# Block 1's input projections reordered, the down projections' last weight piece taken late, and the last tiles finished from PSUM

## The reference

```python
h = rmsnorm(x, attn_norm[l])
c_q, c_kv, k_r, q_d, k_d, v_d = jnp.split(h @ w_in[l], split_at, axis=-1)
o_a = mla_mixer(c_q, c_kv, k_r, cos, sin, g_cq, g_ckv, w_uq, w_ukv, g_mla_q, g_mla_k)
q_d = rmsnorm(q_d.reshape(B, S, DIL_HEADS, DIL_HD), g_dil_q[l])
k_d = rmsnorm(k_d.reshape(B, S, DIL_HEADS, DIL_HD), g_dil_k[l])
o_b = dilated_attention(q_d, k_d, v_d, rel_bias)
x = x + jnp.concatenate([o_a, o_b], -1) @ w_out[l]
x = x + conv_ffn(rmsnorm(x, ffn_norm[l]), w_up[l], conv_w[l], conv_b[l], w_down[l])
```

```python
fx = rmsnorm_2(x, g_pre_ffn[i]) * (1.0 + sc2) + sh2
yx = conv_ffn_2(fx, w_up[i], w_ffn_conv[i], b_ffn_conv[i], w_down[i])
x = x + ga2 * rmsnorm_2(yx, g_post_ffn[i])
```

## Time and profile before

| | |
|---|---|
| three runs | 1769.87, 1771.72, 1773.66 us; median 1771.72 |
| profiled execution | 1769.04 us, of which the profile's span is 1767.3 us |
| granted TensorE clock, mean | 0.973 |
| busy share of the span | PE 93%, PEld 75%, DVE 64%, ACT 48%, POOL 15% |
| DMA | 258.32 MB, mean 146 GB/s |

### The profile page before, as it was taken

One profiled execution on the slowest core, in us unless ns is written; L12 is line 12 of the kernel. 1 busy time (PEld: TensorE's weight loads), 2 busy tenths in 40 slices (PEclk: granted clock), 3 DMA queues, 4 the chain that ended last, 5 costly groups with the idle time before them and its releaser, 6 DMA issues. The chain is left out here.

```text
span 1767.3 us, 22843 instructions
## 1 busy us (share of the span) xinstructions
PE 1639.4 (93%) x8628; PEld 1317.5 (75%) x8628; DVE 1124.4 (64%) x1875; ACT 848.6 (48%) x1518; POOL 262.0 (15%) x322
## 2 busy tenths in 40 slices
PE   7989999999999999899899899999999797989996
PEld 7667887886677887678467588888787595668875
DVE  5686898465868995553673744444333756579964
ACT  5554776355556664431353533333212534566742
POOL 2000113600021117000000001111630000001171
PEclk9999999999999999999999899999999799989998
DMA  7465765554578555523273533333222342246651
GB/s 261 151 209 172 202 189 180 193 167 166 198 225 246 145 170 169 161 78 96 94 237 111 155 96 96 96 96 96 96 95 96 102 138 66 72 124 187 184 185 48
DMA packets 266495, 258.32 MB, mean 146 GB/s; under 512 B 8821, under 2 KB 208729, under 8 KB 266130
## 3 DMA queue, kind: packets, MB, share of 16 engines
q1 hardware_dynamic: 262706, 245.36, 45.7%
q0 software_dynamic: 3536, 11.42, 1.8%
q10 hardware_dynamic: 144, 0.07, 0.0%
HBM read 255.72 MB, written 1.10 MB: 145 GB/s over the span
## 5 line engine op out<-in xcount | busy, mean ns | idle before, releaser
L556 PE MATMUL psv<-hHL,wH 128*128 128x512 f32 (+1 forms) x1952 | 644.2, 392 | 25.0 <-issue 21.1
L1186 DVE TENSOR_TENSOR wL<-ring,wH 128x1024 fp32r<-128x1024 f32 (+2 forms) x364 | 450.5, 1243 | 269.8 <-ACT wH L1761 266.7
L1761 ACT ACTIVATE wH<-ring 128x1024 fp32r<-128x1024 f32 (+2 forms) x364 | 376.1, 1040 | 302.1 <-PE psv L556 295.6
L556 PE MATMUL psv<-hHL,wL 128*128 128x256 f32 (+1 forms) x1504 | 468.5, 311 | 0.0
L556 PEld LDWEIGHTS psv<-hHL,wH 128*128 128x128 f32 x1952 | 368.2, 191 | 108.6 <-issue 23.3
L556 PE MATMUL psv<-wH,hHL 128*128 128x512 f32 (+2 forms) x936 | 319.2, 390 | 30.4 <-DVE wL L1186 17.6
L556 PEld LDWEIGHTS psv<-hHL,wL 128*128 128x128 f32 x1504 | 287.3, 191 | 15.9
L556 PE MATMUL pss<-wH,hHL 128*128 128x512 f32 (+3 forms) x808 | 274.4, 385 | 0.0
L556 PEld LDWEIGHTS psv<-wH,hHL 128*128 128x128 f32 x936 | 175.7, 189 | 74.4 <-DVE wL L1186 24.9
L556 PE MATMUL psv<-wL,hHL 128*128 128x512 f32 (+2 forms) x468 | 180.1, 385 | 0.0
L556 PEld LDWEIGHTS pss<-wH,hHL 128*128 128x128 f32 x808 | 152.5, 190 | 29.4
(11 more groups left out here) (239 smaller groups left out, 1702.3 us busy)
## 6 DMA issues: line engine op xcount, KB each, us to landing
ring<-in_w_up SPq DMA_DIRECT2D x176, 512.0 KB, 5.2
ring<-in_w_mod SPq DMA_DIRECT2D x96, 512.0 KB, 4.8
ring<-in_w_down SPq DMA_DIRECT2D x88, 512.0 KB, 4.3
ring<-in_w_in SPq DMA_DIRECT2D x52, 512.0 KB, 4.6
ring<-in_w_out SPq DMA_DIRECT2D x32, 512.0 KB, 4.7
ring<-in_w_in SPq DMA_DIRECT2D x8, 384.0 KB, 6.0
ring<-in_w_in SPq DMA_DIRECT2D x8, 288.0 KB, 6.9
ring<-in_w_ukv SPq DMA_DIRECT2D x4, 512.0 KB, 4.2
```

Source lines behind the costliest of these rows:

```text
L556: return pe.matmul(o, a, b, start=start, stop=stop, skip_group_check=True)
L1186: v.tensor_tensor(lo, raw, hi.bitcast(F32), ALU.subtract).then_inc(piece_split, told("piece_split", p))
L1761: return ac.activation(o, i, ACT.Copy)
```

## The change

Three things are rearranged; no arithmetic on weights or features is added or removed, apart from the last tiles.

*Input projections of block 1.* TensorE transposes the dilated heads before the bias bands and projection 4, not after them; the squares of the first 128 tokens' MLA heads get room in `W` of their own, so that ScalarE need not wait for the dilated heads. ScalarE splits the third piece of projection 2 ahead of the four latent squares, and does the roots for both tiles in one operation each. Both engines split the third piece of projection 4 earlier. ScalarE loads its Exp table before it empties projection 4. The first two pieces of the output projection are no longer split by VectorE before attention, but at steps p = 8 and 9 of it (`early`); ScalarE makes the first at p = 8 and the second behind its Sqrt table load, where it was. The modulation chunks for attention now come ahead of both `w_out` chunks in the load list.

*Down projections.* With `late`, the first two banks take pieces 19 and 20 before either takes piece 21.

*Last feed-forward.* For its two tiles the squares are summed and the gate is multiplied straight from PSUM, by halves, the updated rows come in halves (`finish`), and the output is stored by SP and ScalarE's queue instead of GpSimd's.

```diff
-        sqm = [w_at(14464, 16, MQK), view(scr, 0, 16, MQK)]
+        sqm = [w_at(10368, 16, MQK), view(scr, 0, 16, MQK)]
...
-            add_cols(A["w_out"][l], 0, 512, ph, "out", 0, between=lambda: add_mod(0, MOD1[l]["pairs"].values()))
+            add_mod(0, MOD1[l]["pairs"].values())
+            add_cols(A["w_out"][l], 0, 512, ph, "out", 0)
...
-            def piece_order(banks, n, tail):
+            def piece_order(banks, n, tail, late=False):
                 m = n - PIECES if tail else n
...
                         yield b, q, w
                     owed.append(piece_used)
                 ws = []
-                for i, b in enumerate(banks):
-                    for q in range(m, n):
-                        if len(ws) < n - m:
-                            ws.append(piece())
-                        yield b, q, ws[q - m]
-                        if i == len(banks) - 1:
-                            owed.append(piece_used)
+                turns = [(i, q) for i in range(len(banks)) for q in range(m, n)]
+                if late:
+                    turns = [(i, q) for i in (0, 1) for q in range(m, n - 1)] + [(0, n - 1), (1, n - 1)] + turns[2 * (n - m):]
+                for i, q in turns:
+                    if len(ws) <= q - m:
+                        ws.append(piece())
+                    yield banks[i], q, ws[q - m]
+                    if i == len(banks) - 1:
+                        owed.append(piece_used)
...
-                for (t, h, kind, b), j, w in piece_order(banks, NJ, True):
+                for (t, h, kind, b), j, w in piece_order(banks, NJ, True, True):
...
+                pe.wait_ge(dil_heads, at("dil_heads", ph))
+                for t in range(NT):
+                    for g in range(2):
+                        transposes("VS"[g], (ph, "dT", t, g),
+                                   [(dqk[:, t, 8 * g + 2 * k:8 * g + 2 * k + 2, :].rearrange("p a b -> p (a b)"),
+                                     slice(k * P, k * P + P)) for k in range(4)])
...
                 project_split(range(NT), [512] * NT, (ph, "in", 4))
-                pe.wait_ge(dil_heads, at("dil_heads", ph))
-                for t in range(NT):
-                    for g in range(2):
-                        transposes("VS"[g], (ph, "dT", t, g),
-                                   [(dqk[:, t, 8 * g + 2 * k:8 * g + 2 * k + 2, :].rearrange("p a b -> p (a b)"),
-                                     slice(k * P, k * P + P)) for k in range(4)])
...
+            sp.wait_ge(residual_updated, at("residual_updated", ("b2", L - 1), "ffn", 0, 1))
+            sp.dma_start(out[0, 0:P, :], xs[:, 0, :]).then_inc(out_stored, mark("out_stored", "all", by=16))
+            sp.wait_ge(residual_updated, at("residual_updated", ("b2", L - 1), "ffn", 1, 1))
+            sp.dma_start(out[0, P:2 * P, 512:D], xs[:, 1, 512:D]).then_inc(out_stored, mark("out_stored", "all", by=16))
+            sp.wait_ge(out_stored, at("out_stored", "all"))
+            sp.wait_ge(half_stored, 16)
...
-            gp.wait_ge(residual_updated, at("residual_updated", ("b2", L - 1), "ffn", 1))
-            for t in range(NT):
-                load(out[0, t * P:(t + 1) * P, :], xs[:, t, :], "out_stored", "all")
-            gp.wait_ge(out_stored, at("out_stored", "all"))
...
+                    if p in early[1]:
+                        splits_to(early[0], p - early[1][0])
...
+                splits_to(first_piece[ph, "in", 4], 2)
+                for t in range(NT):
+                    v.wait_ge(V_full, at("V_full", ph, "dT", t, 0))
+                    b = bank("V", ph, "dT", t, 0)
+                    v.tensor_scalar(dT[:, 0:4, t * P:(t + 1) * P], b[:, :].rearrange("p (k n) -> p k n", k=4),
+                                         col("g_dil_q", l), None, ALU.mult).then_inc(V_free, told("V_free", ph, "dT", t, 0))
...
-                splits_to(first_piece[ph, "in", 4], 2)
...
-                input_rows(4, dvh[:, 0, :, :])
-                for t in range(NT):
-                    v.wait_ge(V_full, at("V_full", ph, "dT", t, 0))
-                    b = bank("V", ph, "dT", t, 0)
-                    v.tensor_scalar(dT[:, 0:4, t * P:(t + 1) * P], b[:, :].rearrange("p (k n) -> p k n", k=4),
-                                         col("g_dil_q", l), None, ALU.mult).then_inc(V_free, told("V_free", ph, "dT", t, 0))
-                splits_to(first_piece[ph, "out", 0], 1)
+                v.wait_ge(V_full, at("V_full", ph, "in", 4, 0))
+                v.tensor_copy(dvh[:, 0, :, :], bank("V", ph, "in", 4, 0)[:, :].rearrange("p (h d) -> p h d", h=8)).then_inc(V_free, told("V_free", ph, "in", 4, 0))
...
-                attention(ph, units1, 0, MOD1[l]["pairs"], mla_columns)
+                attention(ph, units1, 0, MOD1[l]["pairs"], mla_columns, (first_piece[ph, "out", 0], (8, 9)))
...
+                def finish():
+
+                    v.wait_ge(gate_in, at("gate_in", ph, "ffn"))
+                    for t in range(NT):
+                        kind, key = "VS"[t], (ph, "post", "ffn", t)
+                        for h, squares in ((0, key + ("half",)), (1, key)):
+                            n = slice(h * 512, (h + 1) * 512)
+                            v.wait_ge(sum_of_squares, at("sum_of_squares", *squares))
+                            v.tensor_tensor(mixo[:, t, n], bank(kind, ph, "down", t, h), gg[:, 0, n], ALU.mult).then_inc(FREE[kind], told(kind + "_free", ph, "down", t, h))
+                        v.wait_ge(root_ready, at("root_ready", *key))
+                        inverse(rr[:, 4 + t:5 + t], ss[:, 4 + t:5 + t], root[:, 4 + t:5 + t])
+                        v.wait_ge(FREE[kind], at(kind + "_free", ph, "down", t, 1))
+                        for h in range(2):
+                            n = slice(h * 512, (h + 1) * 512)
+                            v.scalar_tensor_tensor(xs[:, t, n], mixo[:, t, n], rr[:, 4 + t:5 + t], xs[:, t, n], ALU.mult, ALU.add).then_inc(residual_updated, told("residual_updated", ph, "ffn", t, h))
...
+                if last:
+                    finish()
+                    continue
...
+            def squares(x, n, c, *key):
+
+                ac.wait_ge(sum_of_squares, at("sum_of_squares", *squared[-1]))
+                squared.append(key)
+                ac.activation(junk[:, 0:n], x, ACT.Square, accum_out=ss[:, c:c + 1]).then_inc(sum_of_squares, mark("sum_of_squares", *key))
+                ac.wait_ge(sum_of_squares, at("sum_of_squares", *key))
...
+                splits_to(first_piece[ph, "in", 2])
                 for base, off, n in ((0, 0, QL), (3, QL, KVL)):
                     for t in range(NT):
                         ac.wait_ge(FREE["VS"[t]], at("VS"[t] + "_free", ph, "in", 1 if base else 0, t))
-                        sumsq(lat[:, t, off:off + n], n, 8 + (2 if base else 0) + t, ph, "lat", base, t)
+                        squares(lat[:, t, off:off + n], n, 8 + (2 if base else 0) + t, ph, "lat", base, t)
+                for f, o in ((ACT.Sqrt, root), (ACT.Identity, ss)):
+                    for c, n in ((8, QL), (10, KVL)):
+                        ins = ac.activation(o[:, c:c + 2], ss[:, c:c + 2], f, scale=1.0 / n, bias=eps_col[:, 0:1])
+                ins.then_inc(root_ready, mark("root_ready", ph, "lat", 3, 1))
...
+                splits_to(first_piece[ph, "in", 4], 2)
...
-                ac.wait_ge(dil_heads, at("dil_heads", ph))
                 for t in range(NT):
                     ac.wait_ge(V_free, at("V_free", ph, "in", 1, 0))
                     ac.wait_ge(S_free, at("S_free", ph, "lift", 3, 1, t))
                     ac.activation(sqm[t], qk[:, t, :, :], ACT.Square).then_inc(head_squares, mark("head_squares", ph, "mla", t))
+                for t in range(NT):
+                    ac.wait_ge(S_full, at("S_full", ph, "dT", t, 1))
+                    b = bank("S", ph, "dT", t, 1)
+                    copy(dT[:, 4:8, t * P:(t + 1) * P], b[:, :].rearrange("p (k n) -> p k n", k=4), col("g_dil_k", l)).then_inc(S_free, mark("S_free", ph, "dT", t, 1))
                 if l == 0:
                     for h in range(1, HEADS, 2):
...
-                input_rows(4, dvh[:, 1, :, :])
-                for t in range(NT):
-                    ac.wait_ge(S_full, at("S_full", ph, "dT", t, 1))
-                    b = bank("S", ph, "dT", t, 1)
-                    copy(dT[:, 4:8, t * P:(t + 1) * P], b[:, :].rearrange("p (k n) -> p k n", k=4), col("g_dil_k", l)).then_inc(S_free, mark("S_free", ph, "dT", t, 1))
-                splits_to(first_piece[ph, "out", 0], 1)
+                splits_to(first_piece[ph, "in", 4] + 3, 0)
+                load_table(ACT.Exp)
+                ac.wait_ge(S_full, at("S_full", ph, "in", 4, 1))
+                copy(dvh[:, 1, :, :], bank("S", ph, "in", 4, 1)[:, :].rearrange("p (h d) -> p h d", h=8)).then_inc(S_free, mark("S_free", ph, "in", 4, 1))
...
-                attention(ph, units1, mla_columns)
```

(19 more changed lines are left out.)

## The result

The changed kernel took 1743.69 us (median of four runs, 1742.57 to 1746.18) beside 1770.8 of the kernel before: ratio 0.9854, 95% interval 0.9835 to 0.9873, or 27.1 us less. The forecast was 1752, range 1746.5 to 1760: the direction was right and the size too small by 8 us. The profiled execution took 1743.62 us (span 1741.8), against the 1749.4 that the sum gave for it: 25.4 us less than before where 19.6 were forecast.

What follows compares the result with a forecast made beforehand. TensorE, busy 93% of the span, was taken as the bound. Projections 2.7 + 7.75, late piece 4.1 and tail 5.0 made 19.6 us: 1769.04 to 1749.4, then 2.7 added for the median gave 1752, range 1746.5 to 1760.

Steps and rivals of the forecast that it cites:

- The tail: End of the last feed-forward: finishing from PSUM, earlier last banks and smaller stores save 5.0 us, bounds 3.3 to 5.5.
- what follows the landing is taken as unchanged: End of the run: the stretch behind the last store's landing was assumed to stay the same, so no gain was counted.
- The half clock: Layer 0, TensorE's 3.43 us pause before the output projection: 1.2 GHz behind it costs 0 or 1.7 us, 0.85 taken.
- The projections: Block 1's input projections and attention, less what is given back: 2.7 us saved in layer 0, 7.75 in layer 1.
- The part for projection 2: Block 1: third weight piece split ahead of the latent squares, so TensorE reaches the fourth 1.9 us earlier per layer.
- the way to the first dilated score: Layer 0, input projections up to attention: VectorE reaches its first dilated score 6.0 us earlier.
- the 2.44 and 1.44 given back: End of block 1's attention: output piece 1's low part delays the output projection, 2.44 us in layer 0, 1.44 in layer 1.
- The late piece: Down projections: last weight piece taken later, every later bank ends 1.36 us earlier; 4.1 us for three, fourth in the tail.
- The step from 1749.4 to 1752: Whole kernel: from profiled execution to median of runs, adding 2.7 us because the profiled execution lay below the median.
- Half of the projections' gain comes back: Rival, block 1: attention lag, half clocks and a late load lose 5 to 9 of 10.4 us; 1757 to 1761, chance 0.22.
- The slower rival: Block 1: output weights loaded behind modulation chunks arrive over 10 us late in each layer; 1775 us, chance 0.03.

Runs made afterwards that it cites:

- that version: The changed kernel with VectorE's low part of the output projection's second piece behind the last split of attention products: 1736.97 us, ratio 0.982; timed again, 1740.28 us.

## Why the prediction was wrong

- **The tail**, forecast 5.0 us, measured 9.9 (8.5 and 1.36): the step that failed first is "what follows the landing is taken as unchanged". GpSimd's drain, 3.82 us in the trace of before, stood behind the landing: 4.24 us from there to the end of the span before, 0.40 after. It is shown by moving the stores both ways. With these 3.8 us the forecast of 1752 would have been some 1748. The rest of the step was near: work to the last issue 3.0 (2.2 and the second issue's 0.6 forecast), landing 1.7 (0.9). Its sum has a slip: a landing of 3.0 for 3.4 and 0.6 for the second issue make 1.0, not the 1.5 that it counts; the measured 2.3 was above either.
- **The half clock**, forecast "The cost is 0 or 1.7; I take 0.85" in layer 0 and nothing in layer 1: 2.56 and 1.6 us in the profile. In the five profiles that have the 3.42 us pause unfilled, the half clock was there each time in layer 0 (1.4 to 2.6 us), and in four of five behind the 1.45 us pause of layer 1. So "0 or 1.7" had a bound that was too low, and layer 1's pause was left out of the sum. The bound came from one execution in which the 2.61 us hole had passed free; in five of six profiles with that hole the half clock followed. The rule of the Trainium skill, "TensorE: Matmul & The Clock Gate", section "HAM oscillation — how this bites in real kernels", weighed there at 1.7 us, pointed the right way.
- **The projections otherwise nearly held.** The part for projection 2 gave 1.6 us in both profiles of the changed kernel (1.9 forecast; the hole left is 1.38 and not 1.1), the way to the first dilated score 5.8 (6.0). With the split in front and no half clock (first profile of that version) they gave 6.2 and 9.7 us (6.0 and 9.2 forecast); the 2.44 and 1.44 given back were measured as 2.4 and 1.45. Layer 0 fell from the forecast 2.7 to 0.5: 1.7 by the half clock behind the pause, the rest ahead of it. Layer 1 fell from 7.75 to 4.8: 1.6 by the half clock behind its pause, some 1.2 by a spell at 0.50 from 542.3 to 545.7, in its up projection, where the first profile of before has none.
- **The late piece**, forecast 4.1 us for three: 1.37 each, as worked out, and 2.3 more in the last mixer behind the third, where the half clock now costs less. The term left out that a shift by 1.36 us changes which products run at half clock. A further 1.3 us went behind the second, but 0.8 went there without the late piece too, so their cause stays open.
- **Chance**: 2.2 us in the last up projection, in neither kernel's code. The bounds, made from the rows of one execution, could not hold it. The step from 1749.4 to 1752 added 2.7 us, since the profiled execution of before lay so far below the median; the changed kernel's lies 0.07 below its own. That is 2.6 of the 8 us.
- **Luck**: the errors go both ways. The projections left 5.3 us of 10.4 while the tail gave 4.9 too much, so that the total is nearer than its parts.
- **The rivals.** "Half of the projections' gain comes back" did come true in size (10.4 forecast, 5.3 left), but not in its time (1757 to 1761). 3.3 of the 5.1 us are the clock behind the two pauses beyond the 0.85 counted; late loads have no part that a trace shows. The slower rival has no trace: in layer 1 ScalarE went from one copy (475.20) straight into output piece 0 (476.38), without a wait for the load:

```profile
475.20 1.09 ACT L1788 ACTIVATE scr<-pss 128x512 f32<-128x512 f32 x2
...
476.38 1.06 ACT L1788 ACTIVATE wH<-ring 128x1024 fp32r<-128x1024 f32 x1
...
478.12 1.08 ACT L1788 ACTIVATE scr<-pss 128x512 f32<-128x512 f32 x2 [0.69 <-PE pss L608]
```

## What to carry to other kernels

Follow the chain past the last landing to the end of the span and look at what each engine's closing instructions cost there; an engine whose close is long should have no part in the last store. When an operation is moved ahead of a split that TensorE waits for, price the pause twice, once as time and once as the half clock behind it, or put the operation behind the split. Before a bound rests on "no slow products here", look at a second execution of the same kernel.

## What was unexpected of the hardware

- GpSimd's closing drain took 3.8 to 3.9 us behind its own stores and 4.5 us when it had issued none at the end; SP's took 0.007 behind its own.
- The 3.42 us pause of TensorE in layer 0 was followed by the 1.2 GHz level in five of five profiles, the 1.45 us pause in layer 1 in four of five, and a pause of 0.99 us in layer 0, where the 3.42 us one stands in the changed kernel, in none of seven. 3.3 us of idle products in place of the 3.42 us pause kept 2.4 GHz behind it.
- The same products (512 columns, last up projection) ran at 391 or 399 ns in the mean in two executions of one program, 2.2 us over the stage.
